# Removing fourteen matmuls with unread results from the mixer of a two-block network on one Trainium2 core

## The reference

```python
x = x + 0.5 * swiglu(rmsnorm(x, ffn1_norm[i]), ...)
h = rmsnorm(x, mix_norm[i]) @ w_in[i]
y_mla = mla_mixer(h[..., OFF_Q:OFF_KV], h[..., OFF_KV:OFF_KPE], ...)   # attention, 8 heads
y_conv = conformer_conv_mixer(h[..., OFF_CONV:OFF_HY], ...)            # depthwise conv, 31 taps
y_hy = hyena_mixer(h[..., OFF_HY:], ...)                               # two long convolutions by FFT
y = jnp.concatenate([rmsnorm(y_mla, ...), rmsnorm(y_conv, ...), rmsnorm(y_hy, ...)], axis=-1)
x = x + y @ w_out[i]
x = x + 0.5 * swiglu(rmsnorm(x, ffn2_norm[i]), ...)
```

## Time and profile before

| what | value |
|---|---|
| median of 3 executions | 3332.11 us (3330.41 to 3334.83) |
| profiled execution, its own time | 3328.09 us |
| span of its instructions | 3326.3 us |
| mean granted TensorE clock | 0.992 |
| busy share TensorE / VectorE / GpSimd / ScalarE | 96% / 49% / 60% / 20% |

### The profile page before, as it was taken

How to read it: one execution, slowest core, us unless ns; L and a number is a source line. 1 busy time by engine, 2 the same in 40 slices (tenths; PEclk the granted TensorE clock), 3 DMA queues, 4 the chain that set the end, 5 groups by cost and what they waited for, 6 DMA issues and landing times.

```text
span 3326.3 us, 44436 instructions
## 1 busy us (share of the span) xinstructions
PE 3207.7 (96%) x14486; PEld 2557.6 (77%) x14486; DVE 1616.7 (49%) x1945; ACT 671.3 (20%) x1215; POOL 2003.1 (60%) x1548
## 2 busy tenths in 40 slices
PE   8999998899999999999889999999999999999998
PEld 6788875478887788886558888788777777778886
DVE  6662268543313656138743331555657786533312
ACT  2110126421101111014541110111122222121100
POOL 6556671266666656674146666755667666776665
PEclk9999999999999999999999999999999999999999
DMA  4223320022233322331012232321222222223322
GB/s 155 83 84 100 111 80 25 19 89 95 95 100 114 97 78 89 99 110 52 14 51 95 95 100 95 117 76 64 70 85 71 76 70 70 89 95 98 98 95 82
DMA packets 77433, 281.28 MB, mean 85 GB/s; under 512 B 9382, under 2 KB 9766, under 8 KB 76776
## 3 DMA queue, kind: packets, MB, share of 16 engines
q1 hardware_dynamic: 74016, 268.58, 25.0%
q10 hardware_dynamic: 3272, 10.79, 0.9%
HBM read 277.24 MB, written 2.10 MB: 84 GB/s over the span
## 4 chain that ended last, share of the span: by engine, by line
PE 84%; DVE 7%; POOL 3%; issue 3%; ACT 1%; DVEq 0%; DMA 0%; ACTq 0%; POOLq 0%; SPq 0%
PE bank L517 25%; PE bank L522 25%; PE bank L521 25%; POOL w_lo L456 3%; PE bank L737 1%; PE bank L652 1%; POOL w_hi L450 1%; PE bank L802 1%; PE bank L831 1%; DVE x_lo L1750 1%; DVE square_sum L1760 1%; DVE xbc L2279 0%; PE bank L811 0%; DVE y L1977 0%; PE bank L631 0%
## 5 line engine op out<-in xcount | busy, mean ns | idle before, releaser
L456 POOL TENSOR_TENSOR w_lo<-raw,w_hi 128x256 fp32r<-128x256 f32 (+1 forms) x1026 | 1433.6, 1418 | 42.0
L450 POOL TENSOR_SCALAR w_hi<-raw 128x1024 fp32r<-128x1024 f32 x504 | 556.6, 1104 | 1250.9 <-PE bank L517 1243.0
L517 PE MATMUL bank<-x_hi,w_hi 128*128 128x512 f32 x2896 | 1151.7, 398 | 49.7 <-DVE x_lo L1750 19.2
L522 PE MATMUL bank<-x_hi,w_lo 128*128 128x512 f32 x2896 | 1131.6, 391 | 0.0
L521 PE MATMUL bank<-x_lo,w_hi 128*128 128x512 f32 x2896 | 1131.0, 391 | 0.0
L517 PEld LDWEIGHTS bank<-x_hi,w_hi 128*128 128x128 f32 x2896 | 545.9, 189 | 195.2 <-issue 80.5
L522 PEld LDWEIGHTS bank<-x_hi,w_lo 128*128 128x128 f32 x2896 | 545.6, 188 | 116.0
L521 PEld LDWEIGHTS bank<-x_lo,w_hi 128*128 128x128 f32 x2896 | 546.3, 189 | 113.8 <-issue 4.1
L517 PE MATMUL bank<-hidden_hi,w_hi 128*128 (+1 forms) x880 | 342.3, 389 | 0.0
L521 PE MATMUL bank<-hidden_lo,w_hi 128*128 (+1 forms) x880 | 342.3, 389 | 0.0
L522 PE MATMUL bank<-hidden_hi,w_lo 128*128 (+1 forms) x880 | 342.3, 389 | 0.0
(11 more groups left out here) (366 smaller groups left out, 2954.5 us busy)
## 6 DMA issues: line engine op xcount, KB each, us to landing
raw<-in_w SPq DMA_DIRECT2D x504, 512.0 KB, 3.5
dft<-in_dft ACTq DMA_DIRECT2D x2, 1536.0 KB, 6.4
out<-x SPq DMA_DIRECT2D x4, 512.0 KB, 2.6
mask<-in_mask ACTq DMA_DIRECT2D x1, 1536.0 KB, 7.1
x<-in_x SPq DMA_DIRECT2D x2, 512.0 KB, 5.4
x<-in_x SPq DMA_DIRECT2D x1, 1024.0 KB, 8.3
filt_cos<-in_dft_filter ACTq DMA_DIRECT2D x2, 512.0 KB, 6.6
filt_sin<-in_dft_filter ACTq DMA_DIRECT2D x2, 512.0 KB, 8.1
```

What stands on the lines that cost most here:

```text
L450: nc.gpsimd.tensor_scalar(w_hi[:, s % 2, :], raw[:, s, :], 1.0, 0.0, ALU.mult, ALU.add).then_inc(w_rounded, 1)
L456: rest = nc.gpsimd.tensor_tensor(w_lo[:, s % 2, at], raw[:, s, at], w_hi[:, s % 2, at].bitcast(F32), ALU.subtract)
L517: first = nc.tensor.matmul(out, hi_w, hi, start=start, stop=False)
L522: return nc.tensor.matmul(out, lo_w, hi, start=False, stop=stop)
```

## The change

All seven pairs go: five calls of `run_idle`, which issue 14 matmuls a layer and 28 in all, and the function itself. The waits that stood in front of the calls at A and E stay, on the instruction behind them or as a wait of their own, or are implied by later ones; the wait on `mixed_copied` at C and D goes from ahead of `turn` and remains in `mix` (h, 0). No other engine's instructions change.

```diff
-            def run_idle(n, to=MIX_BANK, freed=None, by=0):
-
-                if freed is not None:
-                    after(freed, by)
-                for _ in range(2 * n):
-                    nc.tensor.matmul(bank[to][V_DIM:P, 0:CW], ones[:, 0:P - V_DIM], spectrum[:, 0, 0, 0:CW],
-                                     start=True, stop=True)
-
...
                 pe.wait_ge(tile_free, c.at(tile_free) + len(RING))
-                run_idle(1)
                 mla_inputs(0)
                 scores(0, 3)
                 frequencies(0, 1)
                 mla_inputs_taken(0)
-                head(0, lambda: run_idle(2), nothing)
-
-                head(1, lambda: run_idle(1, freed=mixed_copied, by=1), nothing)
+                head(0, nothing, nothing)
+
+                head(1, nothing, nothing)
...
                 def first_inverse():
-                    run_idle(2, HYENA_BANKS[0], spec_free, 4)
                     inverse(1, 0)
 
-                head(5, lambda: run_idle(1, freed=mixed_copied, by=5), first_inverse)
+                head(5, nothing, first_inverse)
```

## The result

The changed kernel takes 3336.46 us (median of 20 executions, 3331.11 to 3339.96), the kernel before 3330.25 us in the same series (20, 3324.51 to 3334.83). The ratio is 1.0018, 95% interval 1.0011 to 1.0025: 6.2 us slower, where 6.0 was forecast.

A forecast was written before the change was run, and what follows sets the result against it. TensorE carries the time (busy 96%), but nothing removed was on the path; clock falls cost A 1.13, C 0.45, E 1.44: 3.0 us a layer, 6.0 in all, added to 3332.11 for 3338 us; 8-in-10 range about 3332 to 3344.5.

The forecast's parts named there:

- A: One pair ahead of `mla_inputs(0)`: removal frees 0, gap grows to 2.9 us; clock-fall chance 0.55, cost 1.13 us a layer.
- E: Two pairs ahead of `inverse(1, 0)`: removal frees 0, gap grows to 2.9 to 3.8 us; clock-fall chance 0.7, 1.44 us a layer.
- C: One pair in head 1, ahead of transposes: removal frees 0; clock-fall chance 0.5 at 0.9 us, 0.45 us a layer.
- D: One pair in head 5, ahead of transposes: they start 0.9 us earlier, VectorE covers; clock falls there already; value 0.
- B: Two pairs in head 0, ahead of transposes: TensorE gets 1.87 us earlier, but VectorE covers; value 0.
- a long fall: Longer stretch at the lower clock: 2.76 us lost where TensorE sets the end, against 1.6 us for the shorter stretch.
- price: Time lost per clock fall where TensorE sets the end: 1.6 to 2.76 us, taken as 2.05.
- No change: Rival: the clock holds in the new gaps or falls only where VectorE covers; 3332 us, chance 0.17.
- faster: Rival: removed matmuls at B, C and D are on the path; 7.6 us gained, 3324.5 us, chance 0.05.
- The long forms everywhere: Rival: every new gap brings the lower clock in both layers, mostly long form; over 10 us, about 3344 us, chance 0.10.
- That transposes don't hold the clock: Rival: gaps at E and C act as longer ones and always fall; 11.4 us, 3343.5 us, chance 0.04.

The follow-up runs named there:

- the two series: The changed kernel (all calls removed) timed twice against the kernel before: 1.0018 (3336.46 against 3330.25 us), then 1.0010 (3333.22 against 3330.12 us).
- the version with five filled gaps: Kernel before with wider fills at A and E, fills in head 3, ahead of head 7's sums and second feed-forward, none at C, D: 0.9976, 3323.72 us.

## Why the prediction was right

*Nothing removed was on the path.* Shown. At B the transposes start 0.64 us earlier by the clock of the profile and 1.94 earlier against their surroundings, which stand 1.30 later for A's fall; 1.87 was forecast. The waits behind are where they were, and twice the calls at B and D changed nothing. At D they start 0.89 earlier against their surroundings, and the wait of TensorE ahead of them is now ended by ScalarE's scaling, as forecast.

*The gaps at A and E grow.* A to 2.8 us, forecast 2.9. E to 2.8 and 2.7 in the changed kernel's first profile and to 3.4 and 3.5 in its second, forecast 2.9 to 3.8.

*The clock falls there by chance, and costs where TensorE sets the end.* Shown in the main: the same program with the same gap at A both fell and held, filled gaps behave otherwise than open ones (A 2 of 10 against 9 of 10), and each fall costs what the products behind it lose, 1.3 to 2.9 us at A and E and nearly nothing at B and C. At E it was less a free throw than the prediction took it for. It lowered E's chance because the clock might still be down from D; in the runs all four falls at E came behind a long fall at D.

*The sizes.* Here the terms were mis-sized, and the errors cancelled in the sum. A: chance 0.55, measured 0.9, but 0.2 also with the call in place, which I had taken as 0; price 2.05, measured 1.7. That is 0.7 x 1.7 = 1.2 a layer against 1.13. The chance of 0.55 was read from the gaps of 3.1 us and passed over a nearer case in the same trace: the gap of 2.74 us ahead of the second feed-forward, behind which the clock fell in both layers. B's gap got no chance at all; it cost nothing, being covered. E: chance 0.7, measured 0.4 (four of ten, in two profiles of five, so hardly known), price 2.05, measured 1.5: 0.6 against 1.44. B and C together: 0.1 against 0.45; the clock fell there more often than the 0.5 put down for C, but a fall cost far less than 0.9. The sum is 1.9 a layer and 3.8 us in all, against 6.0 forecast. The first series measured 6.2 and the second 3.1; the profile of the first series' kernel threw four falls of four, that of the second one of four. That the measured 6.2 meets the forecast's 6.0 so closely is therefore luck; my estimate from the counts and the two series together is 4 to 5 us.

*The rivals.* No change is excluded by both intervals; faster is excluded by the doubled calls. The long forms everywhere didn't come: one fall of thirteen at A and E was long. That transposes don't hold the clock is not what E's four cases show: all four stood behind a long fall at D, where the open gap of 2.7 to 2.8 us fell each time, and all held. A's four, three of which fell, leave a lesser weight open. That equal gaps of one kernel fell and held, as the two of head 3 did before (3.13 and 3.14 us), came again in the changed kernel's two profiles: behind A the clock fell at 493.0 and 1540.9 in the first, and in the second at 1537.2 alone.

## What to carry to other kernels

A matmul whose result nobody reads was worth its time here where it stood in a wait ahead of a stretch that TensorE sets: with the open gap the clock fell behind A in 9 of 10 cases, with one pair in 2 of 10, and a fall cost 1.7 us in the mean. Ask of each such matmul whether the gap could bring the lower clock, and whether TensorE's speed right behind it matters. Where VectorE set the end behind the gap, the calls were free and useless, and so was their removal: twice the calls at B and D gave a ratio of 1.0001, B, C and D removed 1.0004. The calls that were in the kernel were not the most useful ones: C's and D's were left out of the version with five filled gaps, and it is 8 us faster. Look at the granted clock over the whole span, find the falls in front of dense products, fill those gaps first, and look again, as later gaps may fall instead (9 of 12 in the output projection here, in place of 8 of 44). Take several profiles: the changed kernel threw four falls of four at A and E in one profile and one of four in the next.

## What the runs showed that was not expected

A pair at A doesn't make the clock safe: it fell behind a gap of 1.82 us in 2 of 10 cases, while gaps of 3.4 and 3.5 us at E in another kernel left it up. The length of the gap alone didn't decide, then. Filling the gaps of head 3 and head 7 was followed by falls behind shorter gaps of the output projection, 9 of 12 in place of 8 of 44. And the head's transposes, written as eight instructions of 128 columns, take 1.04 us with one record each, while the four records of a pair of 256-column matmuls take 1.08.
